# Feed-forward's first product: two passes over the weights, every token by Strassen's scheme

## What is computed

```python
x = x + rms_norm(mix, ln1_post_g[l])
hid = jnp.square(jax.nn.relu(rms_norm(x, ln2_pre_g[l]) @ w_ff_in[l]))
x = x + rms_norm(hid @ w_ff_out[l], ln2_post_g[l])
```

## Time and profile before

| | us |
|---|---|
| median of three runs | 2793.87 |
| the profiled execution | 2795.2 |
| its span in the trace | 2793.4 |
| `ff_in` in it, from its first DMA issue to that of `ff_out` | 527.8 |
| PE busy in the span | 2533.9 (91%) |
| DVE, ACT, POOL busy in the span | 1306.7, 863.4, 567.5 |
| granted TensorE clock, mean | 0.955 |

### The profile page before, as it was taken

The page is one execution under the profiler, slowest core; times in us unless marked ns, Lnnn a source line. Parts: engine busy times, 40 slices in busy tenths (PEclk is TensorE's granted clock), DMA queues, the critical chain, the costliest instruction groups (busy, mean ns, idle before and its releaser), DMA issues. The chain is left out here.

```text
span 2793.4 us, 33654 instructions
## 1 busy us (share of the span) xinstructions
PE 2533.9 (91%) x12600; PEld 2113.3 (76%) x12600; DVE 1306.7 (47%) x1688; ACT 863.4 (31%) x1415; POOL 567.5 (20%) x499
## 2 busy tenths in 40 slices
PE   6999999797989997998498894799999979999998
PEld 5888888686879895776287683688888768887887
DVE  5665125265635336887633433744444342234332
ACT  4333323251111115776300332322222142133221
POOL 2352236341212110000520231221121000000000
PEclk9999999898999999999599897999999989999999
DMA  4232212585555643221644554232232273345443
GB/s 142 72 91 87 77 53 106 166 260 185 163 158 170 177 135 144 102 102 68 226 141 147 198 176 168 73 98 79 89 97 79 76 254 103 115 145 206 162 150 106
DMA packets 308213, 373.38 MB, mean 134 GB/s; under 512 B 53240, under 2 KB 234616, under 8 KB 303480
## 3 DMA queue, kind: packets, MB, share of 16 engines
q1 hardware_dynamic: 216152, 293.97, 32.8%
q10 hardware_dynamic: 91936, 77.70, 8.5%
HBM read 251.98 MB, written 119.64 MB: 133 GB/s over the span
## 5 line engine op out<-in xcount | busy, mean ns | idle before, releaser
L2473 PE MATMUL y_ps<-w_hi,hid_hi 128*128 128x512 f32 x768 | 301.7, 393 | 23.9 <-DVE w_lo L2557 16.3
L2473 PE MATMUL y_ps<-w_lo,hid_hi 128*128 128x512 f32 x768 | 300.8, 392 | 0.0
L2473 PE MATMUL y_ps<-w_hi,hid_lo 128*128 128x512 f32 x768 | 300.6, 391 | 0.0
L2563 DVE TENSOR_TENSOR hid_lo<-ff_raw,hid_hi 128x1024 fp32r<-128x1024 f32 x96 | 114.0, 1223 | 320.6 <-ACT hid_hi L2527 320.4
L2527 ACT ACTIVATE hid_hi<-ff_raw 128x1024 fp32r<-128x1024 f32 x96 | 97.3, 1053 | 357.1 <-PE y_ps L2473 330.3
L2114 PE MATMUL ff_ps<-ffx_sums,w_ops 128*128 128x512 f32 x768 | 179.0, 392 | 15.7 <-DVE ffx_sums L2249 15.7
L2114 PE MATMUL ff_ps<-ffx_rest,w_ops 128*128 128x512 f32 x768 | 182.1, 393 | 8.3 <-DVE ffx_rest L2249 8.3
L2473 PEld LDWEIGHTS y_ps<-w_hi,hid_hi 128*128 128x128 f32 x768 | 145.5, 189 | 57.0 <-DVE w_lo L2557 17.8
L2114 PEld LDWEIGHTS ff_ps<-ffx_sums,w_ops 128*128 128x128 f32 x768 | 145.1, 189 | 47.1 <-issue 16.9
L2114 PEld LDWEIGHTS ff_ps<-ffx_rest,w_ops 128*128 128x128 f32 x768 | 145.7, 190 | 39.2 <-issue 8.7
L115 PE MATMUL proj_ps<-ht_hi,win_hi 128*128 128x512 f32 x576 | 172.9, 408 | 0.0
(11 more groups left out here) (255 smaller groups left out, 4899.6 us busy)
## 6 DMA issues: line engine op xcount, KB each, us to landing
ff_raw<-s_hid_s SPq DMA_DIRECT2D x96, 512.0 KB, 4.4
arena<-s_dn_s SPq DMA_DIRECT2D x24, 1024.0 KB, 5.7
s_hid_s<-ff_outs SPq DMA_DIRECT2D x96, 256.0 KB, 2.3
w_raw<-in_w_ff_in SPq DMA_DIRECT2D x16, 1024.0 KB, 5.7
ff_raw<-in_w_ff_out SPq DMA_DIRECT2D x32, 512.0 KB, 4.6
win_raw<-in_w_in SPq DMA_DIRECT2D x26, 512.0 KB, 3.4
s_made_s<-arena SPq DMA_DIRECT2D x12, 1024.0 KB, 5.5
arena<-s_made_s SPq DMA_DIRECT2D x48, 256.0 KB, 6.4
```

The costliest lines, as they stand in the source:

```text
L2473: mm = pe.matmul(acc[:, bank(u, t)], x[:, (t if opens(t) else kh), k], y[:, w], start=w == 0 and first == 0, stop=w == KF - 1 and first == 2)
L2563: dve.tensor_tensor(hlo[:, b, ks].rearrange("p k j -> p (k j)"), raw[:, r], f32(hhi[:, b, ks]).rearrange("p k j -> p (k j)"), ALU.subtract ...
```

## The change

The third group's plain products go. The 1536 tokens are now two passes of 768, and each pass is two halves of 384 tokens, so that all tokens go through the seven half products. A pass goes over all 16 pairs, so the weights are loaded twice and their sums, high and low parts are made twice: 32 units of 7 x 12 = 84 matmuls, each of 384 columns. The operands of a pass are all in one tile, `ffx_ops`. The weight buffer `raw` stays single, and so do `w_ops` and `sums`.

- Operands per unit: seven in place of eight (A21 alone is used by no product now; it still goes into the sums).
- Relu squared of C22, C21 and C12 moves from DVE to ACT, as a relu and then a square in place (`relu2` of ACT); that of C11 stays on DVE.
- T3 and T4 are made by DVE and no longer by POOL. Those of the second pass are made in units 4, 6, 8 and 10 of the first pass, behind the unit's last `low`; the rounding of the second pass's operands stands in the last unit of the first pass, one `prep` behind each `low`, on ACT and on DVE.
- SP: one load and four stores per unit. At the start the four quadrants of the first pass are loaded in a row, in place of one quadrant and the slices of the third group; those of the second pass are loaded in unit 1.

The core of the diff (declarations, the views and the lines of `before` that are only taken away are left out):

```diff
+    PASSES = 2
+    UNITS = PASSES * PAIRS
+    WIDE = TOK // (2 * PASSES)
...
+        x_ops = c.sb("ffx_ops", [P, 7, 2, HK, WIDE], F32R)
         raw = c.sb("w1_raw", [P, KD, 2 * P])
-        w_ops = c.sb("w1_ops", [P, 8, 2, HK, P], F32R)
+        w_ops = c.sb("w1_ops", [P, 7, 2, HK, P], F32R)
...
+                def load_weights(x):
+                    if x:
+                        sp.wait_ge(s["w_lo"], 7 * x)
+                    i = x % PAIRS
                     sp.dma_start(raw[:], io["w_ff_in"].rearrange("(k p) n -> p k n", p=P)[:, :, i * 2 * P:(i + 1) * 2 * P]).then_inc(s["w_in"], 16)
...
+                load_tokens(0)
+                for x in range(UNITS):
+                    p, i = divmod(x, PAIRS)
+                    if x + 1 < UNITS:
+                        load_weights(x + 1)
+                    if i == 1 and p + 1 < PASSES:
+                        load_tokens(p + 1)
+                    for o in (C11, C22, C21, C12):
+                        if o == C11:
+                            sp.wait_ge(s["curved"], x + 1)
                         else:
+                            sp.wait_ge(s["squared"], 3 * x + o)
...
+                for x in range(UNITS):
+                    p, i = divmod(x, PAIRS)
+                    for q in range(7):
+                        if 7 * x + q >= 8:
+                            pe.wait_ge(*used(*divmod(7 * x + q - 8, 7)))
+                        pe.wait_ge(s["w_lo"], 7 * x + q + 1)
                         if i == 0:
+                            pe.wait_ge(s["x_lo"], 7 * p + q + 1)
                         for k in range(HK):
+                            for n, (a, b) in enumerate(((0, 0), (0, 1), (1, 0))):
+                                mm = pe.matmul(bank(x, q), w_ops[:, LEFT[q], a, k], x_ops[:, RIGHT[q], b, k], start=k == 0 and n == 0,
+                                               stop=k == HK - 1 and n == 2)
+                        mm.then_inc(s["product"], 1)
...
+                    act.activation(p1[:], bank(x, P1), ACT.Copy).then_inc(s["p1_done"], 1)
+                    for q in range(7):
+                        if more:
+                            high(x + 1, q)
+                            if i == 0:
+                                prep(p, q)
+                        if q == P7:
+                            relu2(x, C22, "c22_made")
+                            relu2(x, C21, "c21_made")
+                    relu2(x, C12, "c12_made")
...
+                for x in range(UNITS):
+                    p, i = divmod(x, PAIRS)
+                    done(dve, x, P2)
+                    dve.wait_ge(s["p1_done"], x + 1)
+                    out_free(dve, x, C11)
+                    dve.tensor_tensor(outs[:, C11], p1[:], bank(x, P2), ALU.add).then_inc(s["c11_made"], 1)
+                    following(x, P1)
+                    dve.wait_ge(s["c11_made"], x + 1)
+                    dve.scalar_tensor_tensor(outs[:, C11], outs[:, C11], 0.0, outs[:, C11], ALU.max, ALU.mult).then_inc(s["curved"], 1)
+                    following(x, P2)
+                    done(dve, x, P6)
...
+                    dve.tensor_tensor(u2[:], p1[:], bank(x, P6), ALU.add).then_inc(s["u2_done"], 1)
+                    following(x, P5)
...
+                    dve.tensor_tensor(u4[:], u2[:], bank(x, P5), ALU.add).then_inc(s["u4_done"], 1)
+                    following(x, P6)
+                    done(dve, x, P7)
...
+                    dve.tensor_tensor(u2[:], u2[:], bank(x, P7), ALU.add).then_inc(s["u3_done"], 1)
...
+                    dve.tensor_tensor(outs[:, C22], u2[:], bank(x, P5), ALU.add).then_inc(s["c22_made"], 1)
...
+                    dve.tensor_tensor(outs[:, C21], u2[:], bank(x, P4), ALU.subtract).then_inc(s["c21_made"], 1)
+                    following(x, P4)
+                    following(x, P7)
+                    done(dve, x, P3)
...
+                    dve.tensor_tensor(outs[:, C12], u4[:], bank(x, P3), ALU.add).then_inc(s["c12_made"], 1)
+                    following(x, P3)
+                    if p + 1 < PASSES and i in (4, 6, 8, 10):
+                        token_sum(p + 1, (i - 4) // 2)
```

More of the change, by code:

```diff
@@ L1997, in ff_in @@
     HK = KD // 2
[L1998 to L2002, removed]
+    C11, C22, C21, C12 = range(4)
     with ExitStack() as ctx:
         c = Core(nc, ctx, "ff_in")
[L2005 to L2009, removed]
+        front = c.sb("ffx_raw", [P, 8, HK, WIDE])
+        x_ops = c.sb("ffx_ops", [P, 7, 2, HK, WIDE], F32R)
@@ L2017, in ff_in @@
         ps = c.ps("ff_ps", [P, 8, 512])
-        names = ("w_in", "s_made", "w_hi", "w_lo", "x_hi", "x_lo", "t_made", "t_pool", "product", "p1_done", "u2_done", "u3_done", "u4_done", "c11_made", "c22_made", "c21_made",
-                 "c12_made", "r_out", "squared", "curved")
+        names = ("w_in", "s_made", "w_hi", "w_lo", "t_made", "x_hi", "x_lo", "product", "p1_done", "u2_done", "u3_done", "u4_done", "c11_made", "c22_made",
+                 "c21_made", "c12_made", "curved", "rectified", "squared")
@@ L2084, in _ @@
-                load_weights(0)
[L2085 to L2099, removed]
-                        else:
[L2101 to L2105, removed]
@@ L2106, in _, with load_tokens @@
-                for u in range(OUTS):
-                    sp.wait_ge(out_stored[u], 16 * (6 * PAIRS // OUTS))
+                def load_tokens(p):
+                    if p:
+                        sp.wait_ge(s["x_lo"], 7 * p)
+                        sp.wait_ge(s["t_made"], 4 * p)
+                    for n, slot in enumerate((2, 0, 3, 1)):
+                        kh, half = QUADRANT[n]
+                        tok = p * 2 * WIDE + half * WIDE
+                        sp.dma_start(front[:, slot], io["ht_s"][kh * HK:(kh + 1) * HK].rearrange("k p t -> p k t")[:, :, tok:tok + WIDE]).then_inc(x_in[n], 16)
@@ new lines, in _ @@
+                load_weights(0)
+                load_tokens(0)
[8 more added lines that the diff above has]
+                            sp.wait_ge(s["curved"], x + 1)
+                        else:
+                            sp.wait_ge(s["squared"], 3 * x + o)
+                        tile, half = {C11: (0, 0), C22: (1, 1), C21: (1, 0), C12: (0, 1)}[o]
+                        t0 = (p * 2 + half) * WIDE // P
+                        sp.dma_start(io["hid_s"][t0:t0 + WIDE // P, :, 2 * i + tile].rearrange("t p j -> p t j"),
+                                     outs[:, o].rearrange("p (t j) -> p t j", j=P)).then_inc(out_stored[o], 16)
@@ L2109, in _ @@
+                for o in range(4):
+                    sp.wait_ge(out_stored[o], 16 * UNITS)
             @block.tensor
             def _(pe):
[L2112 to L2120, removed]
@@ L2134, in remainder @@
[L2134 to L2137, removed]
-                        for k in range(HK):
[L2139 to L2152, removed]
-                    product(i, P3, S4, ("b", B22))
@@ L2171, in _, with done, out_free, flat @@
+            def done(eng, x, q):
+                eng.wait_ge(s["product"], 7 * x + q + 1)
+            def out_free(eng, x, o):
+                if x:
+                    eng.wait_ge(out_stored[o], 16 * x)
+            def flat(a):
+                return a.rearrange("p k t -> p (k t)")
             @block.scalar
             def _(act):
-                def high(i, op):
-                    operand_ready(act, i, op)
-                    act.activation(w_ops[:, op, 0], source(op), ACT.Copy).then_inc(s["w_hi"], 1)
@@ L2192, in relu2 @@
-                def relu2(i, o, q):
-                    done(act, i, q)
-                    out_free(act, i, o)
-                    dst = outs[:, slot(i, o)]
-                    act.activation(dst, bank(i, q), ACT.Relu).then_inc(s["r_out"], 1)
-                    act.wait_ge(s["r_out"], 2 * i + (o == O_R1) + 1)
-                    act.activation(dst, dst, ACT.Square).then_inc(s["squared"], 1)
-                high(0, A11)
-                for n in range(HK):
-                    prep(n)
-                high(0, A12)
@@ L2204, in _, with high @@
-                for n in range(HK, HK + KD + 1):
-                    prep(n)
-                high(0, S1)
-                prep(HK + KD + 1)
-                prep(HK + KD + 2)
-                high(0, S2)
-                prep(HK + KD + 3)
-                high(0, S3)
-                high(0, A22)
-                prep(HK + KD + 4)
-                high(0, A21)
-                prep(HK + KD + 5)
-                high(0, S4)
-                for i in range(PAIRS):
-                    more = i + 1 < PAIRS
-                    done(act, i, P1)
-                    if i:
-                        act.wait_ge(s["u2_done"], i)
-                    act.activation(p1[:], bank(i, P1), ACT.Copy).then_inc(s["p1_done"], 1)
-                    relu2(i, O_R0, R0)
-                    if more:
-                        for op in (A11, A12, S1, S2, S3):
-                            high(i + 1, op)
-                    relu2(i, O_R1, R1)
```

(107 more changed lines are left out.)

191 lines of the change are left out of this document (29 added, 162 removed).

## The result

The changed kernel takes 2913.56 us (median, 2904.74 to 2917.54) against 2793.98: a ratio of 1.0422, 95% interval 1.0397 to 1.0447. It is slower, as forecast, and 18.6 us above the forecast 2895, inside the range. The profiled execution took 2910.99 us with a span of 2909.2.

What follows compares the result with a forecast made beforehand. The weights' turn, 18.6 us against PE's 14.56 a unit, was taken as the bound. `ff_in`: 38 + 30 turns x 18.6 + 10 + 22.4 = 628 us against 527.8, +100.6, so 2895; range 2860 to 2930.

Steps and rivals of the forecast that it cites:

- the turn of the weights: `ff_in`, one weight landing to the next: put at 18.6 us against PE's unit of 14.56, so it sets the pace.
- signs named: Trace after: loads 18 to 19 us apart, PE idle about 4 us a unit, DVE without idle, matmuls near 173 ns.
- change of pass: Unit 15 of `ff_in`: seven low parts of tokens, 1.75 us each, enter DVE's chain, six ahead of C12; +10 us once.
- landing: Weight load's issue until the first engine starts on it: 5.97 us in the late turn, 5.81 in the steady part.
- landing to C12: DVE's chain: one `low` goes (-0.60), relu squared of C22 and C21 leaves (-1.20), steps get narrower (0.133 each).
- tail: End of C12 to the next load: ACT's relu and square (1.4 us) replace DVE's 1.2, so +0.2 a turn.
- start, to the second landing: `ff_in` startup: 32 us until the second load is free to go, which lands at 38.
- from the last landing to the end: End of `ff_in`: first low part 1.9, PE 14.6, waits 1.4, C12 to the store's landing 4.5; 22.4 us.
- The rival without a collision: DVE's four long steps lose 3.25 us without POOL beside them: turn 15.3, so 2796, no change; chance 0.05.
- PE's price: A 384-column matmul in `ff_in`: 173.3 ns (bounds 160 and 226.6), so a unit of 84 takes 14.56 us.
- The rival in which it costs: Clock falls in PE's new gaps: 320 ns a matmul, unit 26.9 us, 3150 if it never came back; chance 0.03.
- The faster rival: PE still sets the pace in `ff_in` if the turn is below 14.56 us: phase 492 us, 2758 in all; chance 0.04.

## Why the prediction was right

**The bound.** Right in place and kind: the turn of the weights, not PE. Two buffers give back 150 us, leaving out a third of the matmuls 12, most of it by landings. Of the signs named, DVE's chain has no idle time, and loads follow 18.8 to 19.9 us apart (from the third on, the change of pass aside). PE's idle time was put at some 4 us a unit and is 3.1: where the clock has fallen in a gap, the matmuls behind it take longer and fill a part of what would be idle.

**The turn** was put at 18.6 and is 19.0. By pieces, from the same working: landing 5.81 (steady part) or 5.97 (late turn of the earlier trace rows), measured 6.02 in the median and 6.09 in the mean; landing to C12 12.93 - 0.60 - 1.20 - 6 x 0.133 = 10.33, measured 10.51; tail 2.32 + 0.20 - 0.13 = 2.39, measured 2.44. The 18.6 stands for a landing halfway, 5.89. **The mis-sized terms are the landing** (0.20 a turn in the mean, 6 us in thirty) **and the chain** (0.18, 5 us); of the chain's 0.18, 0.12 lie in the `low` of S1 beside POOL, 1.30 us where the earlier trace rows have 1.18. In the kernel after, the last three stores are issued within 2.9 us right ahead of the load (first line of the turn above); with the load ahead of the last of them the landing was 5.78. But it was 5.76 too where only matmuls were left out and the stores stood as before, so their part in it is not shown, and what moves a landing by 0.25 us stays open.

**The sum by parts** (us):

| | put at | measured |
|---|---|---|
| start, to the second landing | 38 | 37.8 |
| 30 turns | 558 | 571 |
| change of pass | 10 | 10.1 (29.07 between two loads, less 19.0) |
| from the last landing to the end | 22.4 | 23.3 |
| `ff_in` | 628 | 642.3 |

The median lies 18.6 us above the forecast. The phase makes 14 of them, and the turns 13 of these 14; 1.3 are the other phases (2.1 behind it, less 0.8 ahead of it); the rest is within the spread of the runs after (12.8 us).

**DVE and POOL.** The scalar_tensor_tensor went from 1.78 to 1.63 us, 0.15 less, where standing still and then being short gave 0.13 and a slowing in proportion 0.45. The price of all four long steps, 3.25 by the rows, is 3.31 by experiment. The rival without a collision was put at 2796; the kernel with one-column sums measures 2812, and most of the 16 us between are its turns, which took 473 us where 459 were put.

**PE's price.** 72 matmuls in a row took 12.72 us at full clock in the trace after (first line below), and one lies 0.334 us long (the mean with two buffers), so (12.72 - 0.334) / 71 = 174 ns, with 173.3 forecast. With two buffers the unit is 14.56, which is 84 x 173.3 ns; so the 13.3 ns beside the columns did stay as they were. The estimate by the Trainium skill ("TensorE: Matmul & The Clock Gate", section "Back-to-back issue gap"), 13.65 us a unit, is not what this kernel shows. That section of the Trainium skill gives the formula for an isolated matmul and, for a stream of weight loads and matmuls, about 131 ns at 512 columns; the 226.6 ns of the kernel before is above both.

```profile
1998.61 12.72 PE L2097 MATMUL ff_ps<-ffx_ops,w_ops 128*128 128x384 f32 x72 [0.91 <-DVE w_ops L2163]
...
2013.00:2016.00 3.00, 1.70 (x5) 1.73 (x6) 3.00 (x3) 1.70 (x4) 2.92 (x3) 0.56 0.00 0
```

**The clock.** It did fall in some of the gaps: the second line, of the busy time by stretch, shows 0.56 around the gap of 2.97 us at 2014, and the 84 matmuls behind it took 17.53 us in place of 14.7. They ended before the next low part came (2031.87 + 1.21), and DVE's chain in this turn stood still for no product, so it cost nothing. The rival in which it costs is also refuted by the kernel with two thirds of the matmuls, whose mean clock over the span is the lowest (0.920) and whose time is shorter.

**The faster rival** was not wrong in its time: at PE's pace it was put at 2758, and two buffers run at 2764. It only lacked the buffer.

## What to carry to other kernels

Cutting an engine's work also cuts the cover that it gave: before halving a unit, write down the longest loop that is hidden behind it (load, prepare, combine, store, next load) and measure it where it is not hidden, such as right after a start. If the loop is longer than the new unit, the loop is the new price; here a second buffer of 8 KB a partition turned +4.2% into -1.0%. A queue that issues loads behind stores ties the two together, and each step of a strictly ordered engine between them counts in full.

## What was not expected of the hardware

The landing of a 1 MB load, in the median of thirty, was 6.02 and 6.01 us in the two traces of the changed kernel, 6.06 without the sums and 6.00 with relu squared on DVE, but 5.76 with two thirds of the matmuls and 5.78 with the load ahead of a store. The runs don't show why.

In the changed kernel a granted clock of 0.50 came after PE gaps of some 3 us, in about every second unit and not in each. In the kernel without sums the gaps were below 1 us, and the clock stayed at 1.00 from 1768 to 1986.
